# Three layout turns move from TensorE to VectorE and DMA, and two branches of the output projection change places

## The reference

```python
y = _rms(h, norm_mix_g);  z = y @ w_in                 # (256, 4096)
za, zb, zc, zd = jnp.split(z, split_at, axis=-1)       # 1024, 1536, 1024, 512 columns
oa = _mixer_sgu(za, ...)         # u * (causal 128x128 product of LN(v) + b), 4 heads of 128
ob = _mixer_shortconv(zb, ...)
oc = _mixer_conformer(zc, ...)   # a*sigmoid(g) -> causal conv, 31 taps, + bias -> LN -> silu
od = _mixer_pool(zd, ...)
h = h + jnp.concatenate([oa, ob, oc, od], axis=-1) @ w_out      # (2048 x 2048)
```

## Time and profile before

| what | value |
|---|---|
| time, median of 3 runs | 1419.76 us (1418.84 to 1419.98) |
| time of the profiled execution | 1419.42 us |
| its span, first to last instruction | 1417.7 us, so 1.7 us lie around it |
| PE busy | 1411.9 us (100%) |
| DVE busy | 892.4 us (63%) |
| ACT busy | 715.7 us (50%) |
| DMA | 318.07 MB, mean 224 GB/s |
| granted TensorE clock | 1.000 |

### The profile page before, as it was taken

One profiled execution on the slowest core, in us unless ns is written; L12 is line 12 of the kernel. 1 busy time (PEld: TensorE's weight loads), 2 busy tenths in 40 slices (PEclk: granted clock), 3 DMA queues, 4 the chain that ended last, 5 costly groups with the idle time before them and its releaser, 6 DMA issues.

```text
span 1417.7 us, 17668 instructions
## 1 busy us (share of the span) xinstructions
PE 1411.9 (100%) x6367; PEld 1158.9 (82%) x6367; DVE 892.4 (63%) x1091; ACT 715.7 (50%) x982; POOL 78.6 (6%) x64
## 2 busy tenths in 40 slices
PE   9999999999999999999999999999999999999999
PEld 7888888888888888888888888888888887777887
DVE  5589976665545555455555445556767759896653
ACT  7477755554444433444434344345556647665442
POOL 2000010000000000000000000000000134330000
PEclk9999999999999999999999999999999999999999
DMA  9777657676766656676666667667768688889752
GB/s 330 246 207 223 197 179 252 222 252 194 223 223 223 221 195 195 193 222 223 224 198 219 193 192 224 189 228 237 249 229 281 200 280 249 259 270 299 249 196 89
DMA packets 171734, 318.07 MB, mean 224 GB/s; under 512 B 11953, under 2 KB 35757, under 8 KB 171544
## 3 DMA queue, kind: packets, MB, share of 16 engines
q1 hardware_dynamic: 156792, 285.37, 62.0%
q10 hardware_dynamic: 13088, 25.18, 5.6%
q0 software_dynamic: 1792, 6.71, 1.4%
HBM read 293.04 MB, written 24.17 MB: 224 GB/s over the span
## 4 chain that ended last, share of the span: by engine, by line
PE 97%; DMA 1%; DVE 1%; ACT 1%; issue 0%; POOL 0%; SPq 0%; ACTq 0%
PE acc L1556 31%; PE acc L1557 31%; PE acc L1558 31%; PE acc L1618 1%; PE sp L1760 1%; PE tp L1776 1%; DVE w_lo L1009 0%; PE tp L1576 0%; DMA parked<-wide 0%; ACT w_hi L658 0%; DMA wide<-parked 0%; DMA w_raw<-in_w_in 0%; POOL rs L594 0%; PE sp L1687 0%; PE sp L1608 0%
## 5 line engine op out<-in xcount | busy, mean ns | idle before, releaser
L1009 DVE TENSOR_TENSOR w_lo<-w_raw,w_hi 128x1024 fp32r<-128x1024 f32 x488 | 598.9, 1230 | 483.2 <-ACT w_hi L658 481.9
L658 ACT ACTIVATE w_hi<-w_raw 128x1024 fp32r<-128x1024 f32 x500 | 528.6, 1060 | 635.7 <-PE acc L1558 632.7
L1556 PE MATMUL acc<-w_lo,yh 128*128 128x512 f32 x1056 | 411.2, 389 | 0.0
L1557 PE MATMUL acc<-w_hi,yh 128*128 128x512 f32 x1056 | 410.8, 389 | 0.0
L1558 PE MATMUL acc<-w_hi,yl 128*128 128x512 f32 x1056 | 410.8, 389 | 0.0
L1556 PE MATMUL acc<-w_lo,hh 128*128 128x512 f32 x784 | 307.5, 392 | 0.0
L1558 PE MATMUL acc<-w_hi,hl 128*128 128x512 f32 x784 | 305.2, 389 | 0.0
L1557 PE MATMUL acc<-w_hi,hh 128*128 128x512 f32 x784 | 305.2, 389 | 0.0
L1556 PEld LDWEIGHTS acc<-w_lo,yh 128*128 128x128 f32 x1056 | 198.2, 188 | 42.0 <-issue 0.6
L1558 PEld LDWEIGHTS acc<-w_hi,yl 128*128 128x128 f32 x1056 | 198.2, 188 | 41.3
L1557 PEld LDWEIGHTS acc<-w_hi,yh 128*128 128x128 f32 x1056 | 198.2, 188 | 40.8
(11 more groups left out here) (167 smaller groups left out, 702.5 us busy)
## 6 DMA issues: line engine op xcount, KB each, us to landing
w_raw<-in_w_gate SPq DMA_DIRECT2D x88, 512.0 KB, 3.9
w_raw<-in_w_up SPq DMA_DIRECT2D x88, 512.0 KB, 3.9
w_raw<-in_w_down SPq DMA_DIRECT2D x88, 512.0 KB, 3.7
w_raw<-in_w_in SPq DMA_DIRECT2D x64, 512.0 KB, 4.6
w_raw<-in_swa_w_in ACTq DMA_DIRECT2D x48, 512.0 KB, 5.4
w_raw<-in_w_out SPq DMA_DIRECT2D x32, 512.0 KB, 4.5
w_raw<-in_w_ple_gate SPq DMA_DIRECT2D x32, 512.0 KB, 5.2
w_raw<-in_swa_w_out SPq DMA_DIRECT2D x32, 512.0 KB, 4.2
```

Of the source, the lines that this page charges most:

```text
L658: act.activation(w_hi[:, s % SPL], w_raw[:, s % RAW], ACT.Copy).then_inc(hi_ready, 1)
L1009: dve.tensor_tensor(w_lo[:, s % SPL], w_raw[:, s % RAW], w_hi[:, s % SPL].bitcast(F32), ALU.subtract).then_inc(lo_ready, 1)
L1556: pe.matmul(dst, xh[:, f, tk], w_lo[:, s % SPL, k], start=(f == 0), stop=False)
L1557: pe.matmul(dst, xh[:, f, tk], w_hi[:, s % SPL, k], start=False, stop=False)
```

## The change

- The three turns of the conformer and sgu branches leave TensorE's order. The convolution's result, its normalised form and the gated sgu output become the trips M_CB, M_CN and M_OA: two DVE transposes each, one write and four reads by SP.
- M_CB's transposes stand at (7, 4) in DVE's order, before the sgu statistics; their data is read back into tile[0] by token. DVE takes the statistics from there behind the split of chunk 64, normalises and transposes behind the split of chunk 65, where before all of this stood behind the split of chunk 67.
- M_OA's transposes follow the gating at (0, 0).
- SP issues the writes behind the loads of chunks 68, 74 and 77 and the reads behind those of 70, 76 and 78.
- ACT waits for M_CN's data behind the split of chunk 71 (before: for PE's transposes, behind that of chunk 69), applies silu, waits for itself and copies; it waits for M_OA's data behind the split of chunk 73.
- The conformer moves to hh[8:12] and the sgu branch to hh[12:16], so PE uses the conformer in chunks 72 and 73 and the sgu branch in 74 and 75 of the first column group; `OUT_ROWS` follows.

Context lines are cut.

```diff
@@ -45,7 +45,7 @@
 IN_ORDER = (6, 5, 2, 4, 3, 7, 1, 0)
 U_G, U_A, U_H, U_CG, U_BG, U_D, U_V, U_U = range(8)
-OUT_ROWS = (4, 6, 12, 14, 0, 2, 8, 10)
+OUT_ROWS = (4, 6, 12, 14, 8, 10, 0, 2)
 SWA_ORDER = (4, 0, 1, 2, 3, 5, 6, 7, 8)
@@ -82,9 +82,9 @@
 LAST_CHUNK[SO_UNIT] = START[SO_UNIT] + 14
-HALVES = "d" + "xx" * 4 + "d" + "dx" + "aa" + "xx" + "dd" + "aa" + "xx"
-H_MIX, H_X, H_VEC, H_INIT, H_PZ, H_PO, H_CB, H_CN, H_OA = 0, 1, 9, 10, 12, 14, 16, 18, 20
-M_HC, M_SC, M_BG = range(3)
+HALVES = "d" + "xx" * 4 + "d" + "dx" + "aa" + "xx"
+H_MIX, H_X, H_VEC, H_INIT, H_PZ, H_PO = 0, 1, 9, 10, 12, 14
+M_HC, M_SC, M_BG, M_CB, M_CN, M_OA = range(6)
 H_SWA = len(HALVES)
 HALVES += "xx"
@@ -168,7 +168,7 @@
     x_v = x.rearrange("b (t p) n -> p (b t) n", p=P)
...
     parked = nc.dram_tensor("parked", (P, 1024), F32, kind="Internal").ap()
-    parked_m = [nc.dram_tensor(f"parked_m{i}", (P, 1024), F32, kind="Internal").ap() for i in range(3)]
+    parked_m = [nc.dram_tensor(f"parked_m{i}", (P, 1024), F32, kind="Internal").ap() for i in range(6)]
     parked_p = [nc.dram_tensor(f"parked_p{i}", (P, 1024), F32, kind="Internal").ap() for i in range(4)]
     with ExitStack() as ctx:
@@ -278,7 +278,7 @@
         bias_sb = sem("bias_sb")
...
         sgu_sum = sem("sgu_sum")
-        oa_ready = sem("oa_ready")
+        silu_done = sem("silu_done")
         pooled = sem("pooled")
...
         q_squares = sem("q_squares")
@@ -391,11 +391,11 @@
         def turned_tile(n):
             return turn_buffers(n)[1].rearrange("p (q k t n) -> p k t q n", q=4, k=4, t=T)
-        mixed = [wide[:, 0, 1024 * i:1024 * (i + 1)] for i in range(2)]
+        mixed = [wide[:, 0, 0:1024], wide[:, 0, 1024:2048], wide[:, 0, 0:1024], tile[0][:], tile[0][:], tile[1][:]]
         lag_tile = [wide[:, 1, 1024 * i:1024 * (i + 1)].rearrange("p (k n) -> p k n", k=4) for i in range(2)]
         def mixed_tile(i):
-            return mixed[i % 2].rearrange("p (q k t n) -> p k t q n", q=4, k=4, t=T)
+            return mixed[i].rearrange("p (q k t n) -> p k t q n", q=4, k=4, t=T)
         def quarters(dst):
             return dst.rearrange("p k (t q n) -> p k t q n", t=T, q=4)
@@ -444,12 +444,12 @@
             def put_mixed(i):
                 sp_.wait_ge(mix_blocks, i + 1)
-                sp_.dma_start(parked_m[i][:, :], mixed[i % 2]).then_inc(mix_out, 16)
+                sp_.dma_start(parked_m[i][:, :], mixed[i]).then_inc(mix_out, 16)
             def fetch_mixed(i):
                 sp_.wait_ge(mix_out, 16 * (i + 1))
-                from_quarters(mixed[i % 2], parked_m[i], mixed_in)
+                from_quarters(mixed[i], parked_m[i], mixed_in)
             def put_probs(n):
@@ -480,6 +480,10 @@
             for j in range(NG):
...
                     load(START[OUT_UNIT + j] + c, wout_v, OUT_ROWS[c], CW * j)
+                    if (j, c) in ((0, 0), (0, 6), (1, 1)):
+                        put_mixed(M_CB + ((0, 0), (0, 6), (1, 1)).index((j, c)))
+                    if (j, c) in ((0, 2), (1, 0), (1, 2)):
+                        fetch_mixed(M_CB + ((0, 2), (1, 0), (1, 2)).index((j, c)))
                     if j >= 2 and c == 4:
                         move(T_FFN + j - 2)
@@ -803,21 +807,22 @@
                     split(START[OUT_UNIT + j] + c)
...
                         take(PROJ_UNIT + 1 + c, wide_v[:, :, CW * (c + 1):CW * (c + 2)], ACT.Copy, 1.0)
-                    if (j, c) == (0, 1):
+                    if (j, c) == (0, 3):
                         wait_half_left(act, H_PO + 1)
-                        for i in range(2):
-                            wait_half(act, H_CN + i)
-                            for k in range(2):
-                                f = 2 * i + k
-                                last = act.activation(feat(6)[:, f], half_tile(H_CN + i)[:, k], ACT.Silu,
-                                                      bias=vec[:, V_LB + f:V_LB + f + 1],
-                                                      scale=vec[:, V_LG + f:V_LG + f + 1])
-                            last.then_inc(tp_left["a"], 1)
-                        wait_half_left(act, H_CN + 1)
-                        act.activation(hh[:, 12:16], feat(6), ACT.Copy).then_inc(mix_hi, 1)
-                    if (j, c) == (0, 3):
-                        high(H_OA, hh[:, 8:12])
+                        act.wait_ge(mixed_in, 64 * (M_CN + 1))
+                        for f in range(4):
+                            last = act.activation(quarters(feat(6))[:, f], mixed_tile(M_CN)[:, f], ACT.Silu,
+                                                  bias=vec[:, V_LB + f:V_LB + f + 1],
+                                                  scale=vec[:, V_LG + f:V_LG + f + 1])
+                        last.then_inc(silu_done, 1)
+                        act.wait_ge(silu_done, 1)
+                        act.activation(hh[:, 8:12], feat(6), ACT.Copy).then_inc(mix_hi, 1)
+                    if (j, c) == (0, 5):
+                        act.wait_ge(mixed_in, 64 * (M_OA + 1))
+                        for t in range(T):
+                            last = act.activation(quarters(hh[:, 12:16])[:, :, t], mixed_tile(M_OA)[:, :, t], ACT.Copy)
+                        last.then_inc(mix_hi, 1)
                     if j and c == 4:
...
                         if j == 1:
@@ -1078,7 +1083,7 @@
             def turn_mixed(i, src):
-                into = mixed[i % 2].rearrange("p (r k t n) -> p k r t n", r=4, k=4, t=T)
+                into = mixed[i].rearrange("p (r k t n) -> p k r t n", r=4, k=4, t=T)
                 for t in range(T):
...
                 last.then_inc(mix_blocks, 1)
@@ -1203,6 +1208,12 @@
                         last.then_inc(pooled, 1)
                     if (u, c) == (7, 4):
+                        dve.wait_ge(conv, 4 * TAPS)
+                        into = mixed[M_CB].rearrange("p (q k t n) -> p k q t n", q=4, k=4, t=T)
+                        for t in range(T):
+                            block = feat(1)[:, :, P * t:P * (t + 1)].rearrange("p k (q n) -> p k q n", q=4)
+                            last = dve.transpose(into[:, :, :, t], block)
+                        last.then_inc(mix_blocks, 1)
                         wait_left(dve, U_V)
...
                         for i in range(8):
@@ -1227,19 +1238,28 @@
                             last = dve.tensor_tensor(tok(2)[:, t], tok(2)[:, t], big[:, 512:1024], ALU.add)
                         last.then_inc(sgu_ready, 1)
+            by_token = mixed[M_CB].rearrange("p (x t n) -> p t x n", x=16, t=T)
+            normed = tok(4).rearrange("p t (x n) -> p t x n", x=16)
             for j in range(4):
                 split(START[PROJ_UNIT + j])
-            for t in range(T):
-                wait_half(dve, H_CB + t)
-                last = dve.bn_stats(cst[:, t], tp[(H_CB + t) % 2][:])
-            step(last)
-            for t in range(T):
-                last = dve.bn_aggr(cmv[:, t], cst[:, t])
-            last.then_inc(want, 1)
-            dve.wait_ge(got, R_CONF + 1)
-            for t in range(T):
-                dve.tensor_scalar(tok(4)[:, t], tp[(H_CB + t) % 2][:], cmv[:, t, 0:1], rs[:, R_CONF, t:t + 1],
-                                  ALU.subtract, ALU.mult).then_inc(tp_left["d"], 1)
+                if j == 0:
+                    dve.wait_ge(mixed_in, 64 * (M_CB + 1))
+                    for t in range(T):
+                        last = dve.bn_stats(cst[:, t], by_token[:, t])
+                    step(last)
+                    for t in range(T):
+                        last = dve.bn_aggr(cmv[:, t], cst[:, t])
+                    last.then_inc(want, 1)
+                if j == 1:
+                    dve.wait_ge(got, R_CONF + 1)
+                    for t in range(T):
+                        last = dve.tensor_scalar(normed[:, t], by_token[:, t], cmv[:, t, 0:1],
+                                                 rs[:, R_CONF, t:t + 1], ALU.subtract, ALU.mult)
+                    step(last)
+                    into = mixed[M_CN].rearrange("p (r k t n) -> p k r t n", r=4, k=4, t=T)
+                    for t in range(T):
+                        last = dve.transpose(into[:, :, :, t], tok(4)[:, t].rearrange("p (r k n) -> p k r n", r=4, k=4))
+                    last.then_inc(mix_blocks, 1)
             for j in range(NG):
                 for c in range(8):
@@ -1254,12 +1274,18 @@
                                 last = dve.scalar_tensor_tensor(tok(5)[:, t, cols], sp[t][:, cols],
...
                                                                 ALU.add, ALU.mult)
-                        last.then_inc(oa_ready, 1)
-                    if (j, c) == (0, 2):
+                        step(last)
+                        turn_mixed(M_OA, tok(5))
+                    if (j, c) == (0, 3):
                         dve.wait_ge(mix_hi, 2)
-                        dve.tensor_tensor(hl[:, 12:16], feat(6), hh[:, 12:16].bitcast(F32), ALU.subtract).then_inc(mix_ready, 1)
-                    if (j, c) == (0, 3):
```

(25 more changed lines are left out.)

## The result

The change makes the kernel slightly slower: 1421.26 us in the median of 20 runs (1418.95 to 1424.71) against 1419.45 us of 20 runs of the kernel before (1418.80 to 1420.90), a ratio of 1.0013 with a 95% interval of 1.0007 to 1.0019. By the resolution of 0.2% that the prediction gives, this is no difference, but it has the other sign than the forecast of 1417.6, and the median lies above the range, which ended at 1420.8. The spread of the runs grew from 2.1 to 5.8 us, and that is as much a result as the median.

What follows compares the result with a forecast made beforehand. PE was taken to bound the kernel: a gain of 2.79 us less losses of 0.1 and 0.5 made 2.2 net, so 1417.6 us for the median, with an 8-in-10 range of 1416.6 to 1420.8.

Steps and rivals of the forecast that it cites:

- What bounds the kernel, and what is removed: PE sets the pace; removing its three groups of transposes behind chunks 65, 67 and 69 gains 2.79 us, 2.9 at most.
- M_CB's transposes at (7, 4): They put 1.22 us into DVE's order; split 64 ends at 190.39 and 0.1 us is lost before chunk 64.
- M_CB's trip: Data back at 190.1, wanted by DVE at 190.3: nothing lost, 0.2 us to spare, 2.5 us late as far end.
- Statistics and normalisation: DVE's work ahead of split 66 makes PE stand 0.4 before chunk 66: 0.5 us lost, 1.0 with slow normalisation.
- M_CN's trip: Write lands in 2.8 to 5.3 us, reads take 6.25; before chunk 72 nothing or 0.5 us lost, taken as nothing.
- M_OA's trip: Reads done by 215.5 to 217.9; before chunk 74 nothing or 1.3 us lost, taken as nothing.
- the forecast's limit of 216.6: At ACT's wait for M_OA's data: each microsecond past this time is one of PE's.
- the third: A trip comes late at ACT's wait for M_CN or M_OA; a 12.4 us trip cancels the gain; chance 25%.
- The range: 8-in-10 range of 1416.6 to 1420.8 us, from all hidden up to late trips with 3 us lost.

Runs made afterwards that it cites:

- e9: The changed kernel with e7's output projection order and DVE's splits pulled ahead of its other work; 1416.54 us.
- e1: The changed kernel again, no edit, for a second profile and its spread; 1420.27 us.
- e4: The changed kernel with the gated sgu output turned on TensorE again and the branches in their old places; 1420.46 us.
- e8: Against the kernel before, only the convolution's result goes by DVE and DMA; normalised form and gated output are turned on TensorE; 1419.11 us.
- e2: The changed kernel without the write and reads of M_CN and M_OA, ACT taking the blocks as DVE left them; 1418.86 us.
- e3: The changed kernel with DVE splitting chunk 66 ahead of the normalisation and M_CN's transposes; median 1.5 us above e1's.
- e6: The changed kernel with DVE's split of chunk 64 moved ahead of the sgu normalisation's gain and bias; 1420.54 us.
- e7: The changed kernel with four chunks of the output projection's second column group between chunks 3 and 4 of the first; 1419.09 us.
- e12: The changed kernel once more, no edit, as control on the third chip; 1420.45 us.

## Why the prediction was wrong

- **What bounds the kernel, and what is removed:** right. The forecast had 2.79 to 2.9 us for the turns on PE; e9 gains 2.8 and its span is 1414.8, 2.9 below that of before.
- **M_CB's transposes at (7, 4):** the sum was right for the execution that was profiled (0.1 us lost). What failed is "Split 64 ... ends at 190.39": it takes the phase of DVE from one execution of before. In the 10 traces with the wait for M_BG's reads DVE starts split 60 at 175.7 to 176.3 instead of 175.05, and where the order is that of the change 0.8 to 0.9 us are lost. I had seen that DVE has no gap from 176 on and did not ask what else had arrived late in it. M_CB's trip, with its 0.2 us to spare, came 0.13 us late in e1 and 0.46 in e4.
- **Statistics and normalisation:** sizes right (1.28, 0.25, 1.00), mechanism right (split 66 behind the transposes), one term wrong: "POOL answers 1.09 us after the aggregation, under split 65". The 1.09 was measured with DVE idle. Under a split DVE has POOL's answer 2.0 us after the aggregation (191.97 to 193.94): POOL's first instruction takes 1.07 instead of 0.19 us. These 0.9 us make up nearly all by which the stand before chunk 66, 1.34 to 1.48 us, exceeds the forecast's 0.4. e8 has the statistics behind all splits again, and there POOL needs its 0.19:

```profile
196.25 0.19 POOL L597 TENSOR_SCALAR eps_ms<-cmv 128x2 f32<-128x2 f32 x1 [12.85 <-DVE cmv L1250]
196.53 0.70 POOL L599 TENSOR_TENSOR rs<-eps_ms,minus_half 128x2 f32<-128x2 f32 x1
```

- **M_CN's trip:** this is the step that decided, since without the two late trips (e2) the median is 1418.86, inside the range. The forecast let the write land in 2.8 to 5.3 us, had up to 0.5 us late for M_CN and 1.3 for M_OA from that, and put both at nothing, because "of the writes the middle value is 3.2". M_CN's write took 5.3 to 7.3 us with the broadcast early. The reads, put at 6.25, were about right with 4.9 to 7.2. From the write's issue to ACT's use it was 12.1 us in the first profile, 11.6 in e1, 13.1 in e3, 13.8 in e6, where 11.1 were to be had. The DMA share was 0.79 to 0.87 while the three writes behind the 3.2 ran, and 0.97 and 1.04 in the two halves of 198 to 206 us after the change, where it had been 0.36 and 0.70. I had the three trips as "3 MB more through HBM ... hidden" and did not add them to the loads of the same stretch. Three writes were also a small sample: the trace of before has 38 more writes of this size to HBM by SP, in the first two groups below, whose middle values are higher (4.3 and 6.3 us) and whose longest took 8.1 us.

```profile
parked<-tile SPq DMA_DIRECT2D x26, 512.0 KB, 4.3
...
parked_p<-prob SPq DMA_DIRECT2D x12, 512.0 KB, 6.3
...
parked_m<-wide SPq DMA_DIRECT2D x3, 512.0 KB, 3.2
```

- **M_OA's trip:** its data came at 217.4 in the first profile, 0.8 us past the forecast's limit of 216.6. It cost nothing, because PE was 2.6 us late itself by then.
- **The rivals:** the third, a late trip, is what happened, at the place that was named, and it had 25%. Its 12.4 us for a trip is in the middle of what was measured for M_CN, but it was reckoned from M_OA's date, where it costs 2.2 us; for M_CN it is 1.3 us late, about what was seen. It was taken as an exception, while it is the rule here, and it came on top of the DVE losses.
- **The range:** its upper end of 1420.8 was the late trip alone, with 3 us lost. 13 of the 20 runs lie above that, because the late trip and both DVE losses come together.

In short: 1419.5 - 2.9 + 0.8 (chunk 64) + 1.4 (chunk 66) + 0.1 to 0.2 (restarts) is 1418.9, where e2 and e7 are; the rest up to the 1420.3 and 1420.5 of e1 and e12 is the trips. Why the first 20 runs lie another 0.8 to 1.0 us higher is open: the one trace is of one of the fastest of them. Part of it is probably the six runs in which the clock fell.

## What to carry to other kernels

Work that moves from the engine that bounds the kernel to one that is idle for 37% of the span is free only where that engine's order has idle time ahead of the next date, and a profile shows the phase of one execution: subtract the delays that earlier DMA trips can bring. A round trip through HBM has to be given the longest time measured for any transfer of its kind and size, plus the load that the change itself adds, and a place where its consumer does not stand in front of other urgent work; here 10.9 us more time turned a loss of 0.13% into a gain of 0.20% once DVE's splits came first. Taking away one stand in front of a date that something else sets gains nothing: e3 and e6 gave all of it back.

## What the runs showed of the hardware

- **A small POOL instruction waits for DVE's split.** 128x2 elements took 1.07 us beside a split of 1.19 and ended 0.05 us behind it; with DVE idle they took 0.19. It is 1.07 in all 12 traces with a split beside it. In e3, with two splits in a row, POOL's second instruction took 1.55 instead of 0.70. The Trainium skill (SBUF — State Buffer, "Terms") calls the port pair that DVE and GpSimd share exclusive and "held for the full instruction"; the traces agree in every case. Here it put 0.9 us on a chain that DVE itself was waiting for.
- **A stand of PE can be paid twice.** In the stand of 3.0 us in e3 the granted clock fell to half (1.2 of 2.4 GHz), which cost 1.5 us more, and a stand of 2.82 us in e6 cost nothing more.
- **The same DMA differs between executions of one kernel by a quarter to a third.** M_CN's write took 5.3, 6.6 and 6.7 us in the three traces of the changed kernel, and its reads 6.7, 4.9 and 5.4. A wait on such a trip in a critical order comes with more spread: 5.8 us over 20 runs, 3.3 and 2.2 over 11, and 2.0 without the two trips (e2).
